# Router's choice in rows of eight, and the second mixer's gated values handed over pair by pair

## What is computed

```python
def mixer_rglru(h, ...):                       # second mixer
    gate, xr = jnp.split(h @ w_in, [D_RNN], axis=-1)
    gate = jax.nn.gelu(gate)
    xr = causal_conv(xr, conv_w) + conv_b
    r = jax.nn.sigmoid(einsum('bthi,hij->bthj', xh, w_a) + b_a)
    i = jax.nn.sigmoid(einsum('bthi,hij->bthj', xh, w_x) + b_x)
    log_a = (LRU_C * r) * jax.nn.log_sigmoid(lam)
    a = jnp.exp(log_a)
    b = jnp.sqrt(-jnp.expm1(2.0 * log_a)) * (i * xr)
    _, hseq = lax.associative_scan(combine, (a, b), axis=1)
    return (gate * hseq) @ w_out

def hierarchical_moe(h, ...):                  # router: 4 groups of 8 experts
    g_logits = xt @ w_rg + b_rg
    g_idx = jnp.argmax(g_logits, axis=-1)
    g_prob = take(softmax(g_logits), g_idx)
    e_logits = (xt @ w_re + b_re).reshape(n_tok, 4, 8)
    e_sel = take(e_logits, g_idx)              # the 8 of the chosen group
    top_val, top_idx = lax.top_k(e_sel, 2)
    gates = g_prob * jax.nn.softmax(top_val, axis=-1)
```

## Time and profile before

| | us |
|---|---|
| median of 3 runs | 2131.32 (2128.92 to 2133.59) |
| the profiled execution | 2132.55 |
| its span | 2130.6 |
| TensorE busy | 1886.9 (89%) |
| VectorE busy | 977.3 (46%) |
| ScalarE busy | 675.2 (32%) |
| DMA, main queue | 620 MB, 72.4% of 16 engines |

### The profile page before, as it was taken

The page is one execution under the profiler, slowest core; times in us unless marked ns, Lnnn a source line. Parts: engine busy times, 40 slices in busy tenths (PEclk is TensorE's granted clock), DMA queues, the critical chain, the costliest instruction groups (busy, mean ns, idle before and its releaser), DMA issues.

```text
span 2130.6 us, 32347 instructions
## 1 busy us (share of the span) xinstructions
PE 1886.9 (89%) x14388; PEld 1491.0 (70%) x14390; DVE 977.3 (46%) x1393; ACT 675.2 (32%) x1005; POOL 39.2 (2%) x46
## 2 busy tenths in 40 slices
PE   9987767677998877676789999999999999999999
PEld 8954433444785433333459999989999998999998
DVE  5722110111662100111158668577667666757665
ACT  6300000000651000000045445445446445435443
POOL 0000000000000000000000003000000000300000
PEclk9998998898999988999899999999999999999999
DMA  9799999999959999999976544355544554435551
GB/s 397 306 386 428 428 427 429 427 427 423 383 225 396 428 427 427 428 427 428 426 306 218 181 179 160 134 201 203 189 178 179 195 180 160 179 122 221 191 193 44
DMA packets 61778, 622.48 MB, mean 292 GB/s; under 512 B 6848, under 2 KB 6976, under 8 KB 10560
## 3 DMA queue, kind: packets, MB, share of 16 engines
q1 hardware_dynamic: 61632, 620.32, 72.4%
HBM read 619.24 MB, written 1.05 MB: 291 GB/s over the span
## 4 chain that ended last, share of the span: by engine, by line
PE 66%; DMA 22%; DVE 7%; ACT 2%; issue 1%; SPq 1%; DVEq 0%; ACTq 0%
PE ps L538 14%; PE ps L541 8%; PE ps L499 7%; PE ps L501 7%; PE ps L500 7%; PE ps L761 7%; DMA expert_ring_a<-in_moe_w_down 7%; DMA dense_ring<-in_moe_w_down 7%; PE ps L749 4%; DMA work<-in_moe_w_down 3%; PE ps L738 3%; PE ps L1016 3%; PE ps L772 2%; DMA dense_ring<-in_moe_w_up 2%; DMA spare_place<-in_moe_w_down 2%; DVE w_lo L1437 2%
## 5 line engine op out<-in xcount | busy, mean ns | idle before, releaser
L1437 DVE TENSOR_TENSOR w_lo<-dense_ring,w_hi 128x1024 fp32r<-128x1024 f32 x374 | 441.9, 1222 | 64.3 <-ACT w_hi L1056 63.6
L1056 ACT CAST w_hi<-dense_ring 128x1024 fp32r<-128x1024 f32 x374 | 373.6, 1049 | 24.0 <-PE ps L501 23.2
L538 PE MATMUL ps<-h_both,w_hi 128*128 128x512 f32 x1392 | 351.2, 393 | 1.2 <-DVE h_both L1451 1.2
L538 PEld LDWEIGHTS ps<-h_both,w_hi 128*128 128x128 f32 x1392 | 250.7, 189 | 48.2 <-DVE h_both L1451 3.5
L1765 DVE TENSOR_TENSOR work<-work,ps 128x256 f32<-128x256 f32 x32 | 13.5, 421 | 482.3 <-ACT work L1245 482.3
L499 PE MATMUL ps<-hid_hi,w_hi 128*128 128x256 f32 x704 | 199.3, 283 | 0.6 <-DVE hid_lo L1912 0.6
L541 PEld LDWEIGHTS ps<-h_both,w_lo 128*128 128x128 f32 x1392 | 189.9, 190 | 13.5
L500 PE MATMUL ps<-hid_lo,w_hi 128*128 128x256 f32 x704 | 199.2, 283 | 0.0
L501 PE MATMUL ps<-hid_hi,w_lo 128*128 128x256 f32 x704 | 199.2, 283 | 0.0
L541 PE MATMUL ps<-h_both,w_lo 128*128 128x256 f32 x1392 | 194.1, 282 | 0.0
L499 PE MATMUL ps<-h_both,w_hi 128*128 128x256 f32 x656 | 188.0, 287 | 1.7 <-DVE h_both L1443 1.7
(11 more groups left out here) (282 smaller groups left out, 2779.4 us busy)
## 6 DMA issues: line engine op xcount, KB each, us to landing
dense_ring<-in_dense SPq DMA_DIRECT2D x203, 1024.0 KB, 4.8
expert_ring_a<-in_moe_w_gate SPq DMA_DIRECT2D x20, 2048.0 KB, 42.3
expert_ring_b<-in_moe_w_up SPq DMA_DIRECT2D x20, 2048.0 KB, 41.6
dense_ring<-in_moe_w_gate SPq DMA_DIRECT2D x18, 2048.0 KB, 39.7
expert_ring_a<-in_moe_w_up SPq DMA_DIRECT2D x16, 2048.0 KB, 40.2
dense_ring<-in_moe_w_down SPq DMA_DIRECT2D x16, 2048.0 KB, 35.7
expert_ring_a<-in_moe_w_down SPq DMA_DIRECT2D x15, 2048.0 KB, 44.6
expert_ring_b<-in_moe_w_down SPq DMA_DIRECT2D x14, 2048.0 KB, 45.0
```

Source lines behind the costliest of these rows:

```text
L538: mm(bank[b + f], w[0][:, f, k, :], h_pairs[:, k, :], start=k == 0, stop=False)
L1056: S.copy(half_of(key, f, 0), tile_of(slot(key), key, f)).then_inc(rounded.up(key, f), 1)
L1437: V.tensor_tensor(half_of(key, f, 1), tile_of(slot(key), key, f), half_of(key, f, 0).bitcast(F32), ALU.subtract).then_inc(remainder.up(key ...
```

## The change

All expert sets and the set of groups are laid out as five rows of eight (the four group logits are padded in front with -1e30 to a row of eight). `first_max` then works on all ten rows (two token tiles) at once, so the group's choice and the best expert of every group come out of one pass, the second-best expert of every group out of a second. Two multiplications at the end keep the chosen group's experts. The scratch tiles of the second pass lie in `hid`, which the experts use later. In the second mixer gates(2) moves between the halves of chunk 5; chunk 8's products run by tile k, both halves of each; VectorE takes gated(0) after the second scan pair, and every later gated value right behind its scan, with the `scaled_gate` steps in other places. ScalarE's and SP's orders stay as they are. Core of the diff:

```diff
-    parts.append(("rank_g", np.tile(N_GROUPS - np.arange(N_GROUPS), (P, 1))))
-    parts.append(("rank_e", np.tile(N_EXP - np.arange(N_EXP), (P, 1))))
+    parts.append(("rank", np.tile(PER_GROUP - np.arange(PER_GROUP), (P, 1))))
...
+    rest_of, one2 = (k_view(m[:, 0:TT * ROWS * PER_GROUP], ROWS * PER_GROUP) for m in hid)
...
             for f in range(2):
+                if f and between:
+                    between()
                 PE.wait_ge(remainder, key, f)
...
-                    as_loaded((s, first + j), 1 + j, lambda k: (vec, "gy", k // 2), lru_gate)
+                    (whole_by_rows if j == 0 else as_loaded)((s, first + j), 1 + j, lambda k: (vec, "gy", k // 2), lru_gate)
...
-                    gates(2)
                     gates(3)
                 claim(4 + j, vec, "scaled_gate", j)
-                tile_products(("lru", 4 + j), 4 + j, h_of("lru"))
+                tile_products(("lru", 4 + j), 4 + j, h_of("lru"), between=(lambda: gates(2)) if j == 1 else None)
...
+        def whole_by_rows(key, b, ready, x):
+            w = k_view(slot(key), CHUNK)
+            PE.wait_ge(dense_loaded[place_of[key]], *key)
+            for k in range(KD):
+                PE.wait_ge(*ready(k))
+                for f in range(2):
+                    ins = mm(bank[b][:, f * T:(f + 1) * T], w[:, k, f * P:(f + 1) * P], x[:, k, :], start=k == f == 0, stop=False,
+                             skip_group_check=True)
...
+            V.memset(lg[:, :, 0:PAD_G], NEG).then_inc(vec.up("pad_g"), 1)
...
             convolve(3)
-            scaled_gate(0)
             factors(1)
             lo(("lru", 6))
             more_factors(1)
-            scaled_gate(1)
+            scaled_gate(0)
             factors(2)
             more_factors(2)
             lo(("lru", 7))
+            scaled_gate(1)
             factors(3)
             more_factors(3)
-            for g in range(4):
+            scaled_gate(2)
+            def scan(g):
...
+            scan(0)
+            scan(1)
+            gated(0)
+            scaled_gate(3)
+            gated(1)
+            for g in (2, 3):
+                scan(g)
+                gated(g)
...
+        def first_max(dst, values, mx):
+            def over_row(m):
+                return flat(m).unsqueeze(2).to_broadcast([P, TT * ROWS, PER_GROUP])
+            seq(V.tensor_reduce(flat(mx), rows(values), X, ALU.max))
+            seq(V.tensor_tensor(rows(dst), rows(values), over_row(mx), ALU.is_equal))
+            seq(V.tensor_tensor(rows(dst), rows(dst), C("rank").unsqueeze(1).to_broadcast([P, TT * ROWS, PER_GROUP]), ALU.mult))
+            seq(V.tensor_reduce(flat(row_rank), rows(dst), X, ALU.max))
+            seq(V.tensor_tensor(rows(dst), rows(dst), over_row(row_rank), ALU.is_equal))
...
+            first_max(one1, lg, row_max)
+            seq(V.scalar_tensor_tensor(flat(rest_of), flat(one1), 2 * NEG, flat(lg), ALU.mult, ALU.add))
+            first_max(one2, rest_of, row_max2)
+            seq(V.tensor_tensor(flat(rest_of), flat(one1), flat(one2), ALU.add))
+            in_group = one1[:, :, only_groups]
             for tt in range(TT):
+                ins = V.tensor_tensor(k_view(chosen[:, tt, :], PER_GROUP), k_view(rest_of[:, tt, of_groups], PER_GROUP),
+                                      in_group[:, tt].unsqueeze(2).to_broadcast([P, N_GROUPS, PER_GROUP]), ALU.mult)
+            seq(ins, "chosen", l)
...
-            seq(V.tensor_tensor(col_of[4], col_of[4], col_of[3], ALU.subtract), "second", l)
+            seq(V.tensor_tensor(flat(row_max2), flat(row_max2), flat(row_max), ALU.subtract))
+            seq(V.tensor_tensor(row_max2[:, :, 1:], row_max2[:, :, 1:], in_group, ALU.mult))
+            seq(V.tensor_reduce(col_of[4], row_max2[:, :, 1:], X, ALU.add), "second", l)
```

More of the change, by code:

```diff
@@ L287, in build, with rows, flat @@
     pick, pick_g, spread = wk(TT * P), wk(TT * P), wk(T)
-    lg = k_view(wk(TT * (N_GROUPS + N_EXP)), N_GROUPS + N_EXP)
-    posm, gates, chosen, tmp_e, one1 = (k_view(wk(TT * N_EXP), N_EXP) for _ in range(5))
-    gmx, goh = k_view(wk(TT * 8), 8), k_view(wk(TT * N_GROUPS), N_GROUPS)
-    col_of = [gmx[:, :, i:i + 1] for i in range(8)]
+    ROWS = N_GROUPS + 1
+    PAD_G = PER_GROUP - N_GROUPS
+    lg = k_view(wk(TT * ROWS * PER_GROUP), ROWS * PER_GROUP)
+    posm, gates, chosen = (k_view(wk(TT * N_EXP), N_EXP) for _ in range(3))
+    one1 = k_view(wk(TT * ROWS * PER_GROUP), ROWS * PER_GROUP)
+    rest_of, one2 = (k_view(m[:, 0:TT * ROWS * PER_GROUP], ROWS * PER_GROUP) for m in hid)
+    gmx = k_view(wk(TT * 8), 8)
+    col_of = [gmx[:, :, i:i + 1] for i in range(8)]
+    row_max, row_max2, row_rank = (k_view(wk(TT * ROWS), ROWS) for _ in range(3))
+    only_groups, of_groups = slice(PAD_G, PER_GROUP), slice(PER_GROUP, None)
+    def rows(m):
+        return m.rearrange("p a (r j) -> p (a r) j", j=PER_GROUP)
+    def flat(m):
+        return m.rearrange("p a r -> p (a r)")
     assert at[0] <= 8864
@@ L517, in square_mean, with tile_products @@
             ins.then_inc(products.up("ms", s), 1)
-        def tile_products(key, b, ready, x=h_halves, ks=range(KD)):
+        def tile_products(key, b, ready, x=h_halves, ks=range(KD), between=None):
             w = weights(key)
             for f in range(2):
+                if f and between:
+                    between()
                 PE.wait_ge(remainder, key, f)
@@ L1227, in moe @@
             table(ACTF.Exp)
-            g = lg[:, :, 0:N_GROUPS]
+            g = lg[:, :, only_groups]
             ACT.wait_ge(vec, "shifted", l)
@@ L1669, in lru @@
                     ins.then_inc(vec.up("scan", h), 1)
-                if g == 1:
-                    scaled_gate(2)
-                elif g == 2:
-                    scaled_gate(3)
-                    gated(0)
-                    gated(1)
-            gated(2)
-            gated(3)
+            scan(0)
[6 more added lines that the diff above has]
+                gated(g)
             for g in range(4):
@@ L1711, in route @@
-            first_max(one1, ev, C("rank_e"), N_EXP, col_of[3], col_of[1])
-            seq(V.tensor_scalar(tmp_e, one1, 2 * NEG, None, ALU.mult))
-            seq(V.tensor_tensor(ev, ev, tmp_e, ALU.add))
-            first_max(tmp_e, ev, C("rank_e"), N_EXP, col_of[4], col_of[1])
-            seq(V.tensor_tensor(chosen, one1, tmp_e, ALU.add), "chosen", l)
-            g = lg[:, :, 0:N_GROUPS]
-            seq(V.tensor_tensor(g, g, bc(col_of[0], N_GROUPS), ALU.subtract), "shifted", l)
-            seq(V.tensor_tensor(col_of[4], col_of[4], col_of[3], ALU.subtract), "second", l)
+            first_max(one1, lg, row_max)
@@ L1725, in weigh @@
             DVE.wait_ge(acted, "exp_g", l)
-            seq(V.tensor_reduce(col_of[2], lg[:, :, 0:N_GROUPS], X, ALU.add))
+            seq(V.tensor_reduce(col_of[2], lg[:, :, only_groups], X, ALU.add))
             seq(V.reciprocal(col_of[2], col_of[2]))
@@ L1732, in weigh @@
             seq(V.tensor_tensor(col_of[4], col_of[4], col_of[5], ALU.mult))
-            seq(V.tensor_tensor(gates, one1, bc(col_of[5], N_EXP), ALU.mult))
-            seq(V.tensor_tensor(tmp_e, tmp_e, bc(col_of[4], N_EXP), ALU.mult))
-            seq(V.tensor_tensor(gates, gates, tmp_e, ALU.add))
+            first, second = one1[:, :, of_groups], one2[:, :, of_groups]
+            seq(V.tensor_tensor(first, first, bc(col_of[5], N_EXP), ALU.mult))
+            seq(V.tensor_tensor(second, second, bc(col_of[4], N_EXP), ALU.mult))
+            seq(V.tensor_tensor(first, first, second, ALU.add))
+            seq(V.tensor_tensor(gates, first, chosen, ALU.mult), "gates", l)
         def count(l):
```

20 lines of the change are left out of this document (6 added, 14 removed).

## The result

| | before | changed |
|---|---|---|
| median, us | 2132.25 (4 runs, 2128.92 to 2133.59) | 2117.14 (4 runs, 2117.03 to 2120.74) |
| profiled execution, us | 2132.55 | 2117.18 |
| its span, us | 2130.6 | 2115.2 |

The ratio of changed to before is 0.9933, with a 95% interval from 0.9917 to 0.9949: faster by 15 us. So some 6 us are not in the forecast.

The account below looks back on a forecast made before the run. Expert stages were taken as bound by transfers, so only chains ending idle DMA stretches counted. From 2132.55 us, -5.9 (second mixer) and -3.0 (routings) gave 2123.6 us, range 2119.5 to 2128.5 us.

Parts of the forecast that it names:

- What bounds the kernel now: Whole kernel: expert stages bound by transfers at 426 GB/s; only computed chains ending three idle DMA stretches could shorten the total.
- Routing, up to 'chosen': Both routings: twelve operations at 0.27 us bring "chosen" 1.6 us earlier; first routing's products start 1.5 us earlier; smaller constants cost nothing.
- Term 1: Second mixer: chunk 8 starts 4.75 us earlier, high clock saves 2.65, waits cost 1.5; -5.9 us.
- Rival 1: Second mixer: the clock or gelu takes back half of the gain, 2126.1 us in all; chance 0.20.
- Term 2: Both routings: earlier "chosen" and high clock in one of the two; -3.0 us.
- Rival 4: Routings: operations in rows of eight cost by the row, making the kernel slower, 2142.9 us; chance 0.03.
- Rival 5: Second mixer: chunk 8 could wait for its weights, the gain falling to about 5 us; chance 0.02.
- Rival 2: Both routings at the high clock, -5.9 - 6.0, 2120.6 us; chance 0.15.

Follow-up runs that it names:

- Late gates: Changed kernel with gates(2) put back behind chunk 5's second half: 2118.62 us (4 runs, ratio 0.9943), second mixer's stretch 47.37 us.
- added zeros: Changed kernel with 5 more products of zeros ahead of each routing's first gather: 2116.02 us; with `work` also at a multiple of 256 bytes: 2118.81 us.

## Why the prediction was wrong

**The failed step** is in "What bounds the kernel now" and in "Routing, up to 'chosen'". I wrote that inside an expert stage "nothing computed faster can count" and gave the stages' length no term at all; and I costed "the smaller constants (28 columns)" at nothing, "VectorE waits there for its first load". That looks at the table's load and not at the address of what lies behind it. The rate of a stage that is bound by its transfers was a term of its own: 5.1 us between the two traces, 5.7 over all profiles, 4.4 us in the medians of the kernel before with its rings moved (2130.90 to 2126.52). With the first of these the forecast would have been 2118.5 us (2123.6 - 5.1), 1.3 us above the profiled execution. Of the 6.4 us between forecast and that execution, 5.1 are the rate and 1.7 are the routings; the small rest goes the other way. Why the place changes the rate stays open.

**Term 1, the second mixer, was right**: -5.73 against -5.9. Its parts too: chunk 8 starts 5.08 us earlier (forecast 4.75), and the two chunks are 0.65 us shorter (forecast 1.15, as -2.65 + 1.5), with waits of 0.60 and 0.71 us (forecast 0.4 and 0.9). Chunk 8 began right behind chunk 7, without a wait. Late gates cost 1.55 us, against the 1.76 of the wait that they bring back. Rival 1 did not occur: gelu came in time and the clock held. In every profile with the whole new mixer the stretch is 45.82 to 45.88 us, in all with the old one 51.43 to 51.55.

**Term 2, the routings, had the right mechanism and the wrong luck**: -1.53 and -3.20, together -4.7, against -3.0. The time of an operation from start to start (0.274 us) was the 0.27 taken. The addition-to-counting times were 7.67 and 10.98 us with a high and a low clock (forecast 7.8 and 11.1). "With the first wait gone, the first gather should be at the high level too" is refuted: in five of the 18 new routings without added zeros the clock fell in the gather all the same. And I left out a middle outcome, a low stretch that is over in time or falls in the gather, 18.5 us, which is 8 of these 18. The traces bear out that the outcome varies with the same instructions: 16.9 us in 8, 18.5 in 8 and 20.1 in 2 of the 18.

**Rival 4** (rows of eight cost by the row) fell: 0.24 us for each of the twelve. **Rival 5** did not occur. Rival 2's 2120.6 us was nearest to the result, but for the wrong reason: only one routing had the high clock throughout, and the missing part was the rate.

## What to carry to other kernels

When a change alters the size of any tile in SBUF, work out where the tiles behind it now start, above all those that large transfers write; in a stage bound by transfers 0.6% of the rate is there or gone by 64 bytes, at no cost in code. When two edits come together and the sum is off, cut both traces at the same events and look first at the stretches that nobody meant to change. And give a clock that falls by chance its own table of outcomes from several profiles before one of them is taken for a success.

## What the runs showed of the hardware

**Place in SBUF and the rate of transfers.** With destinations at multiples of 256 bytes the rows shown have 428 and 429 GB/s in stage 0 and 430 in stage 1; at 64 or 128 bytes beside one 425 to 427 in stage 0, 427 and 428 in stage 1. The DMA engines' share is 1.00 or 1.01 in all of them. The Trainium skill ("DMA: Bandwidth & Descriptors", How a descriptor splits into AXI transactions) says that a transaction must start at a multiple of 256 bytes, so that the first one of a descriptor that starts elsewhere begins at the boundary below, and the bytes before the start are fetched without use and still cost beats (of 32 bytes). It speaks of reading; here the reads were the same and the place of the writes moved. The direction agrees. The size is not explained by it: counted in the unused bytes, 64 bytes and 128 bytes would differ, and stage 0 took 457.05 and 457.06 us (stage 1 427.10 and 428.32). No run here shows the transactions themselves, nor shifts other than these two.

**The clock.** In the old mixer the clock fell during TensorE's wait of 4.9 us in all three profiles that have it, and the stretch varied by 0.12 us only. In the routings, whose TensorE work is products of one and of 36 columns, short transposes and zeros, it fell or held from one profile to the next with the same instructions: 16.9, 18.5 or 20.1 us. By an estimate from these times, that alone can spread the time of one kernel by up to 6.4 us over two routings; its nine runs spread by 7.3 (2113.44 to 2120.74).
